# A second ranking over 64 candidate pairs of a head, gate steps four expert units earlier, and the first two value units' coefficients in a place of their own

## The reference, cut to what matters

```
q = (xt @ peer_wq).reshape(n_tok, 8, 2, 128)
s = einsum('thpc,hpnc->thpn', q, peer_subkeys)            # two score rows of 128 keys for each head
top_s, top_i = top_k(s, 16)
cand_s = top_s[:, :, 0, :, None] + top_s[:, :, 1, None, :]  # 16 x 16 = 256 pairs for each head
cand_i = top_i[:, :, 0, :, None] * 128 + top_i[:, :, 1, None, :]
best_s, best_pos = top_k(cand_s, 16)
idx, gates = take_along(cand_i, best_pos), softmax(best_s)
h = gelu(u[idx] . x) * gates                                # 8 heads x 16 experts of each token
out = sum of h * v[idx]
```

## Time and profile before

| | |
|---|---|
| median of 3 runs | 997.02 us (995.62 to 998.21) |
| the profiled execution | 996.73 us |
| its span, first to last instruction | 994.9 us |
| mean granted clock of PE | 0.993 |
| busy: PE, PEld, DVE, ACT, POOL | 978.5, 921.7, 748.8, 628.0, 596.2 us |
| HBM read | 212.89 MB, 215 GB/s over the span |

### The profile page before, as it was taken

The page is one execution under the profiler, slowest core; times in us unless marked ns, Lnnn a source line. Parts: engine busy times, 40 slices in busy tenths (PEclk is TensorE's granted clock), DMA queues, the critical chain, the costliest instruction groups (busy, mean ns, idle before and its releaser), DMA issues.

```text
span 994.9 us, 22627 instructions
## 1 busy us (share of the span) xinstructions
PE 978.5 (98%) x7344; PEld 921.7 (93%) x7344; DVE 748.8 (75%) x1695; ACT 628.0 (63%) x1232; POOL 596.2 (60%) x292
## 2 busy tenths in 40 slices
PE   9999999999999999989999999989999999999997
PEld 8998899999899999989999999989999999999996
DVE  7664663555647898887688888888888887888886
ACT  7773375646556666666888888855555555555553
POOL 3685634677319999979877777853333334433320
PEclk9999999999999999999999999989999999999999
DMA  7463312456545666555555545589888888988871
GB/s 266 143 229 127 127 43 90 143 178 221 184 144 191 211 211 206 207 200 173 193 189 175 174 169 169 186 315 346 321 309 308 314 308 281 341 312 314 312 274 43
DMA packets 61818, 215.02 MB, mean 216 GB/s; under 512 B 7203, under 2 KB 9251, under 8 KB 61644
## 3 DMA queue, kind: packets, MB, share of 16 engines
q1 hardware_dynamic: 51980, 180.04, 51.9%
q0 software_dynamic: 9216, 33.56, 9.0%
q10 hardware_dynamic: 576, 0.82, 0.2%
HBM read 212.89 MB, written 1.06 MB: 215 GB/s over the span
## 4 chain that ended last, share of the span: by engine, by line
PE 95%; DVE 3%; ACT 1%; DMA 0%; issue 0%; ACTq 0%; POOL 0%; DVEq 0%
PE PS L976 21%; PE PS L913 20%; PE PS L981 11%; PE PS L917 11%; PE PS L484 4%; PE PS L485 4%; PE PS L486 4%; PE PS L862 3%; PE PS L494 2%; PE PS L870 2%; PE PS L939 1%; PE PS L940 1%; PE PS L648 1%; PE PS L498 1%; PE PS L903 1%; PE PS L718 1%
## 5 line engine op out<-in xcount | busy, mean ns | idle before, releaser
L1481 POOL TENSOR_TENSOR lo<-raw,hi 128x1024 fp32r<-128x1024 f32 x191 | 459.6, 2414 | 155.4 <-ACT hi L1054 141.1
L913 PE MATMUL PS<-xb,hi 128*128 128x448 f32 x1024 | 236.2, 373 | 2.8 <-ACT arena L1341 2.8
L976 PE MATMUL PS<-xb,hi 128*128 128x448 f32 x1024 | 234.3, 370 | 3.6 <-DVE xb L2117 3.6
L1054 ACT CAST hi<-raw 128x1024 fp32r<-128x1024 f32 x203 | 212.8, 1049 | 34.6 <-DMA raw<-in_u_units 11.9
L976 PEld LDWEIGHTS PS<-xb,hi 128*128 128x128 f32 x1024 | 184.3, 191 | 16.0 <-issue 3.7
L913 PEld LDWEIGHTS PS<-xb,hi 128*128 128x128 f32 x1024 | 184.1, 190 | 15.2 <-issue 3.0
L2136 DVE TENSOR_TENSOR lo<-raw,hi 128x1024 fp32r<-128x1024 f32 x126 | 154.0, 1222 | 26.9 <-ACT hi L1387 26.9
L1424 ACT CAST xb<-arena 128x224 fp32r (+1 forms) x128 | 48.5, 380 | 152.0 <-PE PS L981 148.7
L981 PEld LDWEIGHTS PS<-xb,lo 128*128 128x128 f32 x1024 | 135.7, 192 | 4.2
L917 PEld LDWEIGHTS PS<-xb,lo 128*128 128x128 f32 x1024 | 133.9, 191 | 4.0
L981 PE MATMUL PS<-xb,lo 128*128 128x224 f32 x1024 | 135.7, 274 | 0.0
(11 more groups left out here) (339 smaller groups left out, 1510.9 us busy)
## 6 DMA issues: line engine op xcount, KB each, us to landing
raw<-in_u_units SPq DMA_DIRECT2D x128, 512.0 KB
raw<-in_v_units SPq DMA_DIRECT2D x128, 512.0 KB
raw<-in_w_in_units SPq DMA_DIRECT2D x43, 512.0 KB
raw<-in_w_q_units SPq DMA_DIRECT2D x16, 512.0 KB
raw<-in_w_proj_units SPq DMA_DIRECT2D x8, 512.0 KB
raw<-in_w_out_units SPq DMA_DIRECT2D x8, 512.0 KB
arena<-bias_rows SPq DMA_DIRECT2D x2, 512.0 KB, 4.9
arena<-in_subkeys_t SPq DMA_DIRECT2D x1, 1024.0 KB, 6.0
```

The lines of the kernel that those rows point to most:

```text
L913: mm(o[:, 0:2 * TD].rearrange("p (s t) -> p s t", s=2), hi[:, w, P * k:P * k + P], xb[:, k, :, 0:TD], start=(k == 0), stop=False, skip_gro ...
L976: return mm(PS[:, V_BANKS[c], 0:2 * TD].rearrange("p (s t) -> p s t", s=2), hi[:, (U_V + j) % 4, P * c:P * c + P], xb[:, j % 4, :, 0:TD], ...
L1054: nc.scalar.copy(hi[:, j, :], raw[:, j, :]).then_inc(hi_made, 1)
L1481: nc.gpsimd.tensor_tensor(lo[:, w, :], raw[:, w, :], hi[:, w, :].bitcast(F32), ALU.subtract).then_inc(lo_pool, 1)
```

## The change

The pairs of a head are cut from 256 to 64, in four blocks of rows and columns (`PAIR_BLOCKS`: first row, rows, columns, position): row 0 with 16 columns, rows 1 to 3 with 8, rows 4 to 7 with 4, rows 8 to 15 with 1. The five rounds of searches run over 64 columns. Since a position in the blocks is no longer row times 16 plus column, row and column are worked out by five and six small instructions instead of two and two. The exponentials move four units earlier (`PICKS_AT` 13), and so do the gate steps (`FIRST` = 68: units 68 to 123); units 124 to 127 are multiplied without a gate step. `GATED_UNITS` = 60 counts the units from 68 on, whose gelu stays in PSUM. The coefficients of V0 and V1 go to `first_coef`, in the place of the one-hots `oh2`, which unit 123 uses last; those of all other value units stay in `xb`. V0's last column tile, in bank 5, is multiplied after its other seven, high and low. The memsets of `coef` rows are spread evenly over nine halves.

```diff
-FIRST, SECOND = 72, TD // 4
+SECOND = TD // 4
+FIRST = NKEYS - SECOND - 4
+GATED_UNITS = NKEYS - FIRST
-PICKS_AT = 14
+PICKS_AT = 13
+PAIR_BLOCKS = [(0, 1, 16, 0), (1, 3, 8, 16), (4, 4, 4, 40), (8, 8, 1, 56)]
+PAIRS = 64
...
-        gh, gl = xh[:, 0:4, 0:TD], xl[:, 0:4, 0:TD]
+        first_coef = nc.alloc_sbuf_tensor_at("first_coef", [P, 2, 2, T], F32R, offset=hot_at + 4 * D)
+        coef_slots = [first_coef[:, 0], first_coef[:, 1]] + [xb[:, j] for j in range(4)]
+        def coef_slot(u):
+            return coef_slots[u if u < 2 else 2 + u % 4]
...
-            with pe.Fori(FIRST // 4 + 1, NKEYS // 4) as i:
+            with pe.Fori(FIRST // 4 + 1, NKEYS // 4 - 1) as i:
                 for j in range(4):
                     pe.wait_ge(coef_made, 4 * i + (j - FIRST - 3 + 2))
                     gated_unit(i, j)
+            for j in range(4):
+                pe.wait_ge(coef_made, GATED_UNITS - 4 + j - 3 + 2)
+                expert_unit(NKEYS // 4 - 1, j)
...
             value_ready(0, 0)
-            for c in range(KT):
-                if c == V_BANKS.index(U_BANKS[0]):
-                    pe.wait_ge(coef_made, SECOND + 1)
-                if c == V_BANKS.index(U_BANKS[3]):
-                    pe.wait_ge(coef_made, SECOND + 2)
-                wide_value(0, c, start=True)
-            value_lows(0, lo_pool, LO_POOL_V + 1)
+            for c in range(KT - 1):
+                if V_BANKS[c] in U_BANKS:
+                    pe.wait_ge(coef_made, GATED_UNITS - 1 + U_BANKS.index(V_BANKS[c]))
+                wide_value(0, c, start=True, u=0)
+            pe.wait_ge(lo_pool, LO_POOL_V + 1)
+            for c in range(KT - 1):
+                low_value(0, c, u=0)
+            pe.wait_ge(coef_made, GATED_UNITS + 2)
+            wide_value(0, KT - 1, start=True, u=0)
+            low_value(0, KT - 1, u=0).then_inc(unit_done, 1)
...
-            act.wait_ge(gates_used, SECOND + 2)
-            make_gh(0, 0)
-            make_gh(0, 1)
-            second_half_gelu(SECOND // 4 - 1, 3)
-            act.wait_ge(coef_made, SECOND + 2)
-            with act.Fori(0, GATHERS // 4) as i:
+            for j in range(4):
+                second_right_copy(SECOND // 4, j, last=True)
+                second_half_gelu(SECOND // 4, j - 1)
+                if j == 1:
+                    act.wait_ge(gates_used, SECOND + 2)
+                    for u in range(2):
+                        nc.scalar.copy(coef_slot(u)[:, 0, 0:TD], coef[:, u, :]).then_inc(gh_made, 1)
+            second_half_gelu(SECOND // 4, 3)
+            act.wait_ge(unit_done, U_V)
+            for j in range(2):
+                value_ahead(0, j)
+            act.wait_ge(coef_made, GATED_UNITS + 2)
...
-                    N, columns = len(values), 2048 // len(values)
+                    N, columns = len(values), P if len(values) > HEADS else PAIRS
...
-                for h in range(0, HEADS, 4):
...
+                for i0, rows, cols, at in PAIR_BLOCKS:
+                    shape = [P, HEADS, rows, cols]
+                    last = V.tensor_tensor(cand[:, :, at:at + rows * cols].rearrange("p h (a b) -> p h a b", b=cols),
+                                           first_ps[:, :, i0:i0 + rows].unsqueeze(3).to_broadcast(shape),
+                                           tv4[:, :, 1, 0:cols].unsqueeze(2).to_broadcast(shape), ALU.add)
+                    ranked(128)
...
                     if side == 0:
-                        link(V.tensor_scalar(place, bp, 4, None, ALU.logical_shift_right))
+                        link(V.tensor_scalar(place, bp, 3, None, ALU.logical_shift_right))
+                        link(V.tensor_scalar(bpf, place, 1.0, 0.0, ALU.subtract, ALU.max))
+                        link(V.tensor_scalar(place, bp, 2, None, ALU.logical_shift_right))
+                        link(V.scalar_tensor_tensor(out=row_ps, in0=place, scalar=6.0, in1=bpf, op0=ALU.subtract, op1=ALU.max))
+                        link(V.scalar_tensor_tensor(out=bpf, in0=bp, scalar=48.0, in1=row_ps, op0=ALU.subtract, op1=ALU.max))
                     else:
-                        link(V.tensor_scalar(place, bp, 15, None, ALU.bitwise_and))
-                    link(V.tensor_copy(bpf, place))
+                        link(V.tensor_scalar(row_ps, bp, 16.0, 2.0, ALU.is_lt, ALU.mult))
+                        link(V.scalar_tensor_tensor(out=row_ps, in0=bp, scalar=40.0, in1=row_ps, op0=ALU.is_lt, op1=ALU.add))
+                        link(V.tensor_scalar(bpf, bp, 56.0, 3.0, ALU.is_lt, ALU.mult))
+                        link(V.scalar_tensor_tensor(out=place, in0=row_ps, scalar=4.0, in1=bpf, op0=ALU.mult, op1=ALU.add))
+                        link(V.tensor_tensor(place, bp, place, ALU.bitwise_and))
+                        link(V.tensor_copy(bpf, place))
+                    ranked(1024)
...
-            dve.wait_ge(gates_used, SECOND + 2)
-            make_gl(0, 0)
-            make_gl(0, 1)
-            gated(final, 3, 3)
-            dve.wait_ge(coef_made, SECOND + 2)
+            for j in range(4):
+                second_halves(final, j)
+                gated(final, j - 1, 3 - j)
+                if j == 1:
+                    for u in range(2):
+                        dve.wait_ge(gh_made, u + 1)
+                        V.tensor_tensor(coef_slot(u)[:, 1, 0:TD], coef[:, u, :], coef_slot(u)[:, 0, 0:TD].bitcast(F32),
+                                        ALU.subtract).then_inc(gl_made, 1)
+            gated(final, 3, -1)
+            dve.wait_ge(coef_made, GATED_UNITS + 2)
...
-RANK_FIXED, RANK_PER_UNIT = 190, 2150
+RANK_FIXED, RANK_PER_UNIT = 190, 2110
```

More of the change, by code:

```diff
@@ L448, in _ @@
                 load_value(j, j)
[L450 removed]
+            sp.wait_ge(coef_made, GATED_UNITS + 2)
             for j in range(RAW, 2 * RAW):
@@ L973, in _, with wide_value, low_value @@
                     gated_unit(i, j)
-            def wide_value(j, c, start=False):
+            for j in range(4):
+                pe.wait_ge(coef_made, GATED_UNITS - 4 + j - 3 + 2)
+                expert_unit(NKEYS // 4 - 1, j)
+            def wide_value(j, c, start=False, u=8):
                 return mm(PS[:, V_BANKS[c], 0:2 * TD].rearrange("p (s t) -> p s t", s=2),
-                          hi[:, (U_V + j) % 4, P * c:P * c + P], xb[:, j % 4, :, 0:TD], start=start, stop=False,
+                          hi[:, (U_V + j) % 4, P * c:P * c + P], coef_slot(u + j)[:, :, 0:TD], start=start, stop=False,
                           skip_group_check=True)
-            def low_value(j, c, last=False):
-                return mm(PS[:, V_BANKS[c], 0:TD], value_slot(j)[:, P * c:P * c + P], xb[:, j % 4, 0, 0:TD],
+            def low_value(j, c, last=False, u=8):
+                return mm(PS[:, V_BANKS[c], 0:TD], value_slot(j)[:, P * c:P * c + P], coef_slot(u + j)[:, 0, 0:TD],
                           start=False, stop=last, skip_group_check=True)
@@ L998, in whole_unit @@
                     wide_value(j, c)
-                value_lows(j, lo_dve, 8 * i + (U_V + j + 1 + LO_DVE_V))
+                pe.wait_ge(lo_dve, 8 * i + (U_V + j + 1 + LO_DVE_V))
+                for c in range(KT):
+                    last = low_value(j, c)
+                last.then_inc(unit_done, 1)
             value_ready(0, 0)
-            for c in range(KT):
-                if c == V_BANKS.index(U_BANKS[0]):
-                    pe.wait_ge(coef_made, SECOND + 1)
-                if c == V_BANKS.index(U_BANKS[3]):
-                    pe.wait_ge(coef_made, SECOND + 2)
-                wide_value(0, c, start=True)
-            value_lows(0, lo_pool, LO_POOL_V + 1)
+            for c in range(KT - 1):
[8 more added lines that the diff above has]
+            low_value(0, KT - 1, u=0).then_inc(unit_done, 1)
             value_ready(0, 1)
             for c in range(KT):
-                wide_value(1, c)
-            value_lows(1, lo_pool, LO_POOL_V + 2)
+                wide_value(1, c, u=0)
+            pe.wait_ge(lo_pool, LO_POOL_V + 2)
+            for c in range(KT):
+                last = low_value(1, c, u=0)
+            last.then_inc(unit_done, 1)
             for j in range(2, 8):
@@ L1414, in _ @@
             for j in range(4):
-                second_right_copy(SECOND // 4 - 1, j, last=True)
+                second_right_copy(SECOND // 4 - 1, j)
                 second_half_gelu(SECOND // 4 - 1, j - 1)
@@ L1423, in make_gh @@
                 act.wait_ge(unit_done, 4 * i + (U_V + j - 3))
-                nc.scalar.copy(gh[:, j % 4, :], coef[:, 4 * i + j, :]).then_inc(gh_made, 1)
+                nc.scalar.copy(coef_slot(4 + j)[:, 0, 0:TD], coef[:, 4 * i + j, :]).then_inc(gh_made, 1)
             def value_ahead(i, j):
@@ L1430, in value_ahead @@
                 value_hi(i, j + 2)
-            act.wait_ge(gates_used, SECOND + 2)
-            make_gh(0, 0)
-            make_gh(0, 1)
-            second_half_gelu(SECOND // 4 - 1, 3)
-            act.wait_ge(coef_made, SECOND + 2)
-            with act.Fori(0, GATHERS // 4) as i:
```

(16 more changed lines are left out.)

21 lines of the change are left out of this document (9 added, 12 removed).

## The result

The changed kernel takes **990.37 us** (median of 6 runs, 988.82 to 992.37) against 996.45 beside it: ratio 0.9941, 95% interval 0.9923 to 0.9958. It is faster, as forecast, by 6.1 us where 8 were forecast. The profiled execution took 990.32 us with a span of 988.5, against 996.73 before.

The account below looks back on a forecast made before the run. TensorE (PE) holds 95% of the chain of waits, so only its standstills and slow-clock stretches matter. From the profiled 996.73 us, minus 3.49 (A) and 4.75 (B), is 988.49; plus 0.29 for the median gives 988.8, range 986.6 to 992.0.

Parts of the forecast that it names:

- The searches: DVE's ranking: 64-column searches estimated at 0.22 us each, so DVE catches up at unit 43 and ranking ends at 430.9.
- L2024, taken at 0.94 us: New SBUF-to-SBUF DVE index instruction in the ranking: costs 0.29 to some 2.4 us; at 0.94, 0.6 us late, inside 0.8 spare.
- A hold over a whole low part: L2024 waits out one whole POOL low part, 2.4 us, so ranking ends at 433.1; chance 0.26.
- first rival: L2024 held for a whole POOL low part: A costs 0.88 + 1.5 us, time 990.3 us; chance 0.26.
- A: Ranking's end, where PE waits for ACT's exponential: cost falls from 4.37 to 0.88 us, a gain of 3.49 us.
- The clock: PE's clock should hold at A, since earlier falls came in standstills of 2.8 and 3.6 us; taken 0, bounds 0 and 1.41.
- B: Step from expert to value units: V2 16.89 us after unit 124, POOL waits of 0.6 and 1.15 us; gain 4.75 us.
- What was costed at nothing: Other edits, 0 us: 15 instead of 14 memsets over nine halves, as many PE matmuls, SP's loads of V4 to V7.

Follow-up runs that it names:

- gathers later: Changed kernel with POOL's first four gathers behind the low parts of V0 and V1, not between those of the last four expert units: 993.29 us, ratio 0.9963.
- end after unit 55: Changed kernel with the ranking's end placed after unit 55 again (`PICKS_AT` 14), still 64 pairs: 996.45 us, ratio 0.9997.
- ranking alone: Kernel before, with 64 pairs and the ranking's end after unit 51; gate steps and coefficients as before: 993.52 us, ratio 0.9971.
- L2024 twice: Changed kernel with instruction L2024 written twice, the second directly behind the first: 991.87 us, ratio 0.9950.
- coefficients back: Changed kernel with the coefficients of V0 and V1 back in `xb`, rounded and split behind the last product: 996.41 us, ratio 1.0005.
- two kernels through PSUM without the later gathers: Changed kernel with L2024's group rewritten through PSUM: 989.43 us; the same with four gathers earlier, behind low parts of units 112, 115, 118, 121: 987.27 us.
- gates alone: Kernel before (256 pairs, ranking's end after unit 55), with gates from unit 68 and own place for V0's and V1's coefficients: 999.81 us, ratio 1.0031.

## Why the prediction was right, and where it was short

It forecast 988.8 us in 986.6 to 992.0, and faster; 990.37 came. Step by step:

- **The searches.** They were taken at 0.22 us at 64 columns; a group of eight took 219 ns each, and DVE caught up at unit 43 as laid out. The row, to be set beside the earlier trace rows (count, busy us, mean ns, idle before):

```profile
L1988 DVE FIND_INDEX8 arena<-con,arena 128x8 uint32<-128x64 f32 x8 | 1.6, 219 | 0.0
```

- **L2024, taken at 0.94 us: this is the step that failed.** It has no one price. In the seven profiled executions with this instruction in this place it took 2.42, 0.23, 2.45, 2.40, 0.71, 0.23 and 2.34 us, by how much of a low part was left when it came (the changed kernel twice, gathers later, end after unit 55, ranking alone, L2024 twice, coefficients back). The first tile's copy, near 355 us, fits: 0.23 to 0.31 us in six of these executions, where POOL paused or a low part ended within 0.4 us, and 1.13 us with the ranking alone, where it ended at 356.25, just behind the end of a low part (the fourth of six that take 14.81 us from 346.26, so about 356.1). The range of 0.29 to 2.4 us held but for its lower end (0.23); taking one value inside it, from the nearest row, did not. A hold over a whole low part had a chance of 0.26; four of the seven executions had one. In the profiled execution this first rival happened: 2.35 us at A, where it reckoned 0.88 + 1.5 = 2.38, and 990.32, where it said 990.3.
- **The rest of A**: the exponential's table was loaded by 431.74 (431.65 forecast), and in the execution without a hold A cost 0.85 us (0.88) and the time was 988.74 us (988.8). The forecast is thus what the program does when L2024 finds POOL pausing. That both times agree to 0.1 us is in part luck: the forecast had added 0.29 us because the median of three runs before lay that much above the profiled execution, and the median of six, 996.45, lies 0.28 below it. Without this term the sum gives 988.5, and 990.0 with a hold. Which of the twelve executions were held is known of the two profiled ones alone. Eight of them lie at 989.47 and more, while the runs of each of the two kernels through PSUM without the later gathers lie within 1.1 us; and the two slowest, 992.37 and 993.67, have the lowest mean granted clock, 0.996 against 0.997 to 0.999. That speaks for holds, some with a fall of the clock, and doesn't show them.
- **The clock** stayed up in the profiled execution, as taken. That was not safe to take: behind stops at A of 1.83 (ranking alone), 2.22 (gathers later) and 2.35 us (L2024 twice) it fell, and the next unit started 3.97 to 4.20 us later; behind 2.19 and 2.12 us (coefficients back) it did not, and that took 2.61. A fall thus costs 1.4 to 1.6 us. PE with the gathers later, then with the coefficients back:

```profile
437.29 3.31 PE L922 MATMUL PS<-xb,hi 128*128 128x448 f32 x8 [2.22 <-ACT arena L1356]
```

```profile
435.49 1.89 PE L921 MATMUL PS<-xb,hi 128*128 128x448 f32 x8 [2.12 <-ACT arena L1355]
```

- **B**: V2 was forecast 16.89 us after unit 124 and came at 17.01. The two waits on POOL, by starts of matmuls, are 652.64 - 650.50 - 1.64 = 0.50 us (0.6 forecast) and 656.16 - 653.63 - 7 x 0.206 = 1.09 (1.15). The gathers were the cause, as the kernels that move them show, and the two splits were held (L2180, 2.64 us for two) without PE waiting for them, both as reckoned.
- **What was costed at nothing** did cost nothing: V4 did not wait for its load, nor PE for the 15 memsets. For the memsets it mattered that they were spread over nine halves, as the prediction says: over five they cost 5.2 us of standstill.
- **The sum**: 8.24 us forecast against 6.41; of the 1.83 missing, 1.47 are A (3.49 - 2.02), 0.12 B, and 0.24 lie outside A and B.

The parts do not simply add. The ranking alone gains 0.29%, the gates alone lose 0.31%, and both together gain 0.59%: the shorter ranking pays twice, at A, and by making room for the gates' preparation four units earlier.

## What to carry to other kernels

Where an instruction can be held by one of another engine, give it two prices and a chance for each, taken from where the other engine stands, and not a value between; then look whether it can be written so that it is not held at all, as three instructions with their PSUM operands exchanged were here. A transfer moved off a late engine must be moved to where that engine idles ahead of the need, since the engine that waits for the data holds up all that is queued behind, as DVE did here for 6.10 us. And before a stage is moved earlier, count what must be done between the stage ahead and it: that room can be the gain's condition.
